# Depthwise convolution of a hybrid trunk step: three channel tiles on VectorE and five on TensorE, with shifted copies of the rows

## What is computed

```python
z = h @ p["w_pw1"] + p["b_pw1"]
a, g = jnp.split(z, 2, axis=-1)
u = a * jax.nn.sigmoid(g)
u = conv_depthwise(u, p["w_dw"], taps=31, padding=15) + p["b_dw"]
u = jax.nn.silu(_layernorm(u, p["ln_g"], p["ln_b"]))
return u @ p["w_pw2"] + p["b_pw2"]
```

## Time and profile before

| | |
|---|---|
| device time, median of 3 runs | 1497.93 us (1497.63 to 1500.12) |
| profiled execution, first to last instruction | 1495.2 us |
| own time of the profiled execution | not given apart; the median is 2.7 us above its span |
| PE busy | 1460.0 us (98%) |
| DVE busy | 1166.2 us (78%) |
| ACT busy | 969.1 us (65%) |
| POOL busy | 39.1 us (3%) |
| DMA, mean over the span | 318 GB/s |

### The profile page before, as it was taken

The page is one execution under the profiler, slowest core; times in us unless marked ns, Lnnn a source line. Parts: engine busy times, 40 slices in busy tenths (PEclk is TensorE's granted clock), DMA queues, the critical chain, the costliest instruction groups (busy, mean ns, idle before and its releaser), DMA issues.

```text
span 1495.2 us, 20201 instructions
## 1 busy us (share of the span) xinstructions
PE 1460.0 (98%) x8274; PEld 1232.3 (82%) x8274; DVE 1166.2 (78%) x1137; ACT 969.1 (65%) x979; POOL 39.1 (3%) x41
## 2 busy tenths in 40 slices
PE   6999999999999999999999999999999999999997
PEld 5778899998977888888888888888888888888885
DVE  3565744455897789889979889878888887988997
ACT  2554633433368487777777778787777777777773
POOL 0210000000000100000000000000000000000010
PEclk9999999999999999999999999999999999999999
DMA  9767766756743579999989999989999998999993
GB/s 375 295 231 281 271 220 231 232 175 226 271 156 109 198 271 375 372 389 377 373 348 378 373 372 392 376 334 389 375 377 385 376 375 347 377 372 389 395 403 140
DMA packets 102530, 474.86 MB, mean 318 GB/s; under 512 B 8316, under 2 KB 39180, under 8 KB 53280
## 3 DMA queue, kind: packets, MB, share of 16 engines
q1 hardware_dynamic: 99696, 465.86, 82.4%
q0 software_dynamic: 2160, 6.92, 1.2%
q10 hardware_dynamic: 576, 0.72, 0.2%
HBM read 468.65 MB, written 4.81 MB: 317 GB/s over the span
## 4 chain that ended last, share of the span: by engine, by line
PE 89%; DVE 5%; DMA 3%; ACT 2%; issue 1%; POOL 0%; ACTq 0%; SPq 0%; DVEq 0%; POOLq 0%
PE bank L1686 20%; PE bank L1684 20%; PE bank L1685 20%; PE bank L1690 6%; PE bank L1692 5%; PE bank L1691 5%; PE bank L2229 2%; PE bank L1727 2%; PE bank L2068 2%; DMA raw<-w_in 1%; PE bank L2022 1%; PE bank L2023 1%; PE bank L2024 1%; DVE hid L1378 1%; PE bank L1744 1%; PE bank L2194 1%
## 5 line engine op out<-in xcount | busy, mean ns | idle before, releaser
L1549 DVE TENSOR_TENSOR low<-raw,high 128x2048 fp32r<-128x2048 f32 x333 | 748.8, 2287 | 106.9 <-ACT high L848 104.9
L848 ACT ACTIVATE high<-raw 128x2048 fp32r<-128x2048 f32 x333 | 632.0, 1921 | 101.5 <-DMA raw<-moe 100.4
L1684 PE MATMUL bank<-high,hidH 128*128 128x512 f32 x896 | 349.5, 390 | 0.0
L1686 PE MATMUL bank<-high,hidL 128*128 128x512 f32 x896 | 349.1, 390 | 0.0
L1685 PE MATMUL bank<-low,hidH 128*128 128x512 f32 x896 | 348.6, 389 | 0.0
L1690 PE MATMUL bank<-hidH,high 128*128 128x256 f32 x736 | 211.5, 287 | 3.4 <-DVE hidL L1013 1.3
L1691 PE MATMUL bank<-hidL,high 128*128 128x256 f32 x736 | 208.1, 283 | 0.0
L1692 PE MATMUL bank<-hidH,low 128*128 128x256 f32 x736 | 208.1, 283 | 0.0
L1686 PEld LDWEIGHTS bank<-high,hidL 128*128 128x128 f32 x896 | 168.2, 188 | 35.0
L1684 PEld LDWEIGHTS bank<-high,hidH 128*128 128x128 f32 x896 | 168.2, 188 | 34.7
L1685 PEld LDWEIGHTS bank<-low,hidH 128*128 128x128 f32 x896 | 168.2, 188 | 34.6
(11 more groups left out here) (244 smaller groups left out, 1292.0 us busy)
## 6 DMA issues: line engine op xcount, KB each, us to landing
raw<-moe SPq DMA_DIRECT2D x336, 1024.0 KB, 5.2
raw<-ada_w SPq DMA_DIRECT2D x40, 1024.0 KB, 5.6
raw<-ffn_gu SPq DMA_DIRECT2D x44, 512.0 KB, 5.0
raw<-ffn_down SPq DMA_DIRECT2D x11, 1024.0 KB, 5.0
raw<-ada_first SPq DMA_DIRECT2D x8, 1024.0 KB, 15.0
raw<-w_in SPq DMA_DIRECT2D x8, 1024.0 KB, 8.7
raw<-conv_pw SPq DMA_DIRECT2D x16, 512.0 KB, 5.1
raw<-w_o SPq DMA_DIRECT2D x4, 1024.0 KB, 6.8
```

The costliest lines, as they stand in the source:

```text
L848: a.activation(high[:, m % SPLITS, :], raw[:, n % RAWS, :], ACT.Copy).then_inc(S("high_ready"), 1)
L1549: v.tensor_tensor(low[:, n % RAWS, :], raw[:, n % RAWS, :], high[:, m % SPLITS, :].bitcast(F32), ALU.subtract).then_inc(S("low_ready"), 1)
L1684: pe.matmul(out, xh, wh, start=start, stop=False)
L1686: return pe.matmul(out, xl, wh, start=False, stop=stop)
```

## The change

- DVE convolves three tiles (DVE_TILES = 3), tiles 0 to 2, and PE five, tiles 3 to 7.
- PE's 128 rows hold four taps of 32 channels. For each tile there are GROUPS = 4 groups of 32 channels and ROUNDS = 8 rounds of four taps. One matmul takes 32 columns of weights and writes the 32 partitions of its group; the four groups of a round write the four quarters of one bank, and the eight rounds sum up. That is 32 matmuls a tile in place of 31, with 32 columns of weights each in place of 128.
- The rows for it lie in `shifted`: for shift a and group g, 32 partitions of `uT` are copied by a DMA to partitions 32a to 32a + 31, moved by a tokens. For each pair of tiles (u = 1, 2, 3; u = 1 has one tile) there are 16 such DMAs, shifts 0 and 1 from ACT's queue and shifts 2 and 3 from POOL's.
- The weights of a tile, 128 x 32 x 32, are made by POOL, one instruction a tile, by multiplying the taps into a 32-column identity (five instructions). They stand in POOL's queue ahead of the four small loads (L478). ACT makes no more diagonal matrices.
- On DVE the taps of two tiles alternate: tiles 0 and 1, then 0 and 2, then 1 and 2. After `glu(2)` there are 14 taps in place of 20.
- `sg` moves into tiles 6 and 7 of `hid`, `uT` to the start of the phase's space with rows of 160, and the ring of diagonal matrices goes.

```diff
-DIAGS = 6
+SHIFTS, GROUPS = 4, 4
+CG = P // GROUPS
+ROUNDS = 8
+UROW = P + 32
...
+DVE_TILES = 3
+PE_TILES = KT - DVE_TILES
...
+        tapU = sb("tapU", [P, 2, GROUPS * ROUNDS, CG], where=ph)
...
+        uT = sb("uT", [P, KT, TILES, UROW], where=ph)
+        shifted = sb("shifted", [P, PE_TILES * GROUPS, TILES, UROW], where=ph)
+        tapD = sb("tapD", [P, 3, GROUPS * ROUNDS, CG], where=ph)
...
+        sg = hid[:, KT - UC:KT, :].rearrange("p c (t n) -> p c t n", t=TILES)
...
+        def conv_tiles(u):
+            return max(UC * u, DVE_TILES) - DVE_TILES, UC * (u + 1) - DVE_TILES
+
+        def shift_rows(eng, u, shifts, arrived):
+            i0, i1 = conv_tiles(u)
+            n = (TILES - 1) * UROW + P + SHIFTS * (ROUNDS - 1)
+            for a in shifts:
+                for g in range(GROUPS):
+                    eng.dma_start(
+                        shifted[CG * a:CG * (a + 1), GROUPS * i0 + g:GROUPS * i1:GROUPS].rearrange(
+                            "c q t n -> c q (t n)")[:, :, 0:n],
+                        uT[CG * g:CG * (g + 1), DVE_TILES + i0:DVE_TILES + i1].rearrange(
+                            "c k t n -> c k (t n)")[:, :, a:a + n]
+                    ).then_inc(S(f"{arrived}{u}"), 16)
...
+            pool.wait_ge(S("state_out"), 32)
+            ident32 = const[:, C_ID32:C_ID32 + CG].unsqueeze(1).to_broadcast([P, GROUPS * ROUNDS, CG])
+            for i in range(PE_TILES):
+                c0 = COLS["tap_groups"][0] + i * GROUPS * ROUNDS
+                w = par[:, c0:c0 + GROUPS * ROUNDS].unsqueeze(2).to_broadcast([P, GROUPS * ROUNDS, CG])
+                st.mark(pool.tensor_tensor(tap_weights(i), w, ident32, ALU.mult), "taps_spread")
             for half, p0 in enumerate((64, 96)):
...
+            for u in range(1, 4):
+                pool.wait_ge(S("glu_ready"), UC * (u + 1))
+                shift_rows(pool, u, (2, 3), "late_shifts")
...
+            def shift_ready(u):
+                a.wait_ge(S("glu_ready"), UC * (u + 1))
+                shift_rows(a, u, (0, 1), "early_shifts")
...
             def conv_out(k):
-                a.wait_ge(S("tap_used"), (k - DVE_TILES + 1) * TAPS)
+                a.wait_ge(S("conv_done"), k - DVE_TILES + 1)
...
+                if u >= 2:
+                    shift_ready(u - 1)
                 glu_gate(u)
-
-            for k in range(DVE_TILES, KT):
-                for j in range(TAPS):
-                    i = (k - DVE_TILES) * TAPS + j
-                    if i >= DIAGS:
-                        a.wait_ge(S("tap_used"), i - DIAGS + 1)
-                    st.mark(a.activation(diag[:, i % DIAGS, :], ident, ACT.Copy,
-                                         scale=taps[:, j * KT + k:j * KT + k + 1]), "diag_ready")
-                if k > DVE_TILES:
-                    conv_out(k - 1)
-                    named("pw2", 0, k - DVE_TILES - 1)
+            shift_ready(3)
+
+            conv_out(DVE_TILES)
+            conv_out(DVE_TILES + 1)
+            named("pw2", 0, 0)
+            conv_out(DVE_TILES + 2)
+            named("pw2", 0, 1)
+            conv_out(DVE_TILES + 3)
             conv_out(KT - 1)
...
+            def conv_taps(k0, j0, k1, j1, n):
+                for j in range(n):
+                    conv_tap(k0, j0 + j)
+                    conv_tap(k1, j1 + j)
...
             glu(0)
-            conv_taps((0, 1), 0, 8)
+            conv_taps(0, 0, 1, 0, 8)
...
             glu(1)
-            conv_taps((0, 1), 8, 16)
+            conv_taps(0, 8, 1, 8, 8)
...
             glu(2)
-            conv_taps((0, 1), 16, 26)
+            conv_taps(0, 16, 2, 0, 7)
             glu(3)
-            conv_taps((0, 1), 26, TAPS)
-            rest = tuple(range(2, DVE_TILES))
-            conv_taps(rest, 0, 8)
+            conv_taps(0, 23, 2, 7, 4)
             rows_out(4)
-            conv_taps(rest, 8, 11)
+            conv_taps(0, 27, 2, 11, 4)
             mod_out(4)
-            conv_taps(rest, 11, 25)
+            conv_taps(1, 16, 2, 15, 6)
             named("pw2", 0, 0)
-            conv_taps(rest, 25, TAPS)
+            conv_taps(1, 22, 2, 21, 9)
+            conv_tap(2, 30)
             named("pw2", 0, 1)
...
+            def conv_tile(k):
+                i, u = k - DVE_TILES, k // UC
+                pe.wait_ge(S("taps_spread"), i + 1)
+                pe.wait_ge(S(f"early_shifts{u}"), 16 * 2 * GROUPS)
+                pe.wait_ge(S(f"late_shifts{u}"), 16 * 2 * GROUPS)
+                if i >= 2:
+                    pe.wait_ge(S("conv_pe_ready"), i - 1)
+                for r in range(ROUNDS):
+                    for g in range(GROUPS):
+                        last = pe.matmul(
+                            bank[CG * g:CG * (g + 1), 4 + k % 2, 0:TOK].rearrange("p (t n) -> p t n", t=TILES),
+                            tap_weights(i)[:, g * ROUNDS + r, :],
+                            shifted[:, GROUPS * i + g, :, SHIFTS * r:SHIFTS * r + P],
+                            start=r == 0, stop=r == ROUNDS - 1)
+                st.mark(last, "conv_done")
...
-            cuts = [(k, j) for k in range(DVE_TILES, KT) for j in range(0, TAPS, 6)]
-            for i, (k, j) in enumerate(cuts):
-                conv_taps(k, j, min(j + 6, TAPS))
-                if i == 5:
-                    ada_sum(4)
-                if i >= 6 and i < 9:
-                    ada_piece(5, i - 6)
+            conv_tile(3)
+            conv_tile(4)
+            ada_sum(4)
+            conv_tile(5)
+            ada_piece(5, 0)
+            ada_piece(5, 1)
+            conv_tile(6)
+            conv_tile(7)
+            ada_piece(5, 2)
             pe.wait_ge(S("conv_part"), DVE_TILES * TAPS)
```

More of the change, by code:

```diff
@@ L54 @@
 C_PAIR = C_SEL + 2 * GC
-C_END = C_PAIR + TILES
+C_ID32 = C_PAIR + TILES
+C_END = C_ID32 + CG
+DVE_TILES = 3
+PE_TILES = KT - DVE_TILES
 COLS = {}
@@ L61 @@
                   ("ln_b", KT), ("w_sc", 3 * SCC), ("q_a", 2), ("kv_a", 1), ("head_gain", 4), ("rope_gain", 4 * ROPE),
-                  ("taps", TAPS * KT), ("router", KT * EXPERTS)):
+                  ("taps", TAPS * DVE_TILES), ("tap_groups", PE_TILES * GROUPS * ROUNDS), ("router", KT * EXPERTS)):
     COLS[_name] = (_c, _c + _n)
@@ L65 @@
 NPAR = _c
-DVE_TILES = 5
 PHASE = 12480
@@ L180, in build @@
         ph.close()
+        ph = ExitStack()
+        tapU = sb("tapU", [P, 2, GROUPS * ROUNDS, CG], where=ph)
+        ph.close()
         sb("up_space", [P, 4 * UC * TOK])
@@ L216, in build @@
         ph = ExitStack()
+        uT = sb("uT", [P, KT, TILES, UROW], where=ph)
+        shifted = sb("shifted", [P, PE_TILES * GROUPS, TILES, UROW], where=ph)
+        tapD = sb("tapD", [P, 3, GROUPS * ROUNDS, CG], where=ph)
+        ph.close()
+        ph = ExitStack()
         sb("row_space", [P, 2 * TILES * D], where=ph)
-        uT = sb("uT", [P, KT, TILES, P + 2 * PAD], where=ph)
-        sg = sb("sg", [P, UC, TILES, P], where=ph)
         sq = sb("sq", [P, KT, TOK], where=ph)
-        diag = sb("diag", [P, DIAGS, P], where=ph)
         ph.close()
@@ L327, in pw2_bank, with tap_weights @@
             return m // 2, (m % 2) * TOK
+        def tap_weights(i):
+            return tapU[:, i] if i < 2 else tapD[:, i - 2]
+        def conv_tiles(u):
[11 more added lines that the diff above has]
+                    ).then_inc(S(f"{arrived}{u}"), 16)
         def kept_rows(e):
@@ L1350, in _ @@
             st.do(v.memset(uT[:, :, :, 0:PAD], 0.0), "pads")
-            st.do(v.memset(uT[:, :, :, PAD + P:], 0.0), "pads")
+            st.do(v.memset(uT[:, :, :, PAD + P:UROW], 0.0), "pads")
             def glu(u):
@@ L1364, in glu, with conv_tap @@
                 v.wait_ge(S("glu_ready"), UC * (u + 1))
[L1366 to L1378, removed]
+            summed = {}
+            def conv_tap(k, j):
+                dst = hid4[:, k, :, :]
+                src = uT[:, k, :, j:j + P]
+                w = taps[:, j * DVE_TILES + k:j * DVE_TILES + k + 1]
+                if j == 0:
+                    b = COLS["dw_b"][0] + k
+                    summed[k] = st.mark(v.tensor_scalar(dst, src, w, par[:, b:b + 1], ALU.mult, ALU.add), "conv_part")
+                else:
+                    v.wait_ge(S("conv_part"), summed[k])
+                    summed[k] = st.mark(v.scalar_tensor_tensor(dst, src, w, dst, ALU.mult, ALU.add), "conv_part")
+            def conv_taps(k0, j0, k1, j1, n):
+                for j in range(n):
+                    conv_tap(k0, j0 + j)
+                    conv_tap(k1, j1 + j)
             named("pw1", "a", 1)
@@ L2332, in constants @@
             c[32 * g + tt, C_PAIR + tt] = 1.0
+        c[32 * g:32 * g + 32, C_ID32:C_ID32 + CG] = np.eye(CG)
     return c
@@ L2373, in parameters @@
     put("rope_gain", np.broadcast_to(np.concatenate(rope)[None, :], (P, 4 * ROPE)))
-    put("taps", columns(inp["conv_dw"][0]))
+    dw = np.asarray(inp["conv_dw"][0], dtype=np.float32)
+    put("taps", columns(dw[:, 0:DVE_TILES * P]))
+    grouped = np.zeros((SHIFTS * ROUNDS, PE_TILES * P), np.float32)
```

(3 more changed lines are left out.)

## The result

| | before | after |
|---|---|---|
| device time, median | 1497.93 us (1496.81 to 1500.12, 5 runs) | 1486.36 us (1483.21 to 1493.24, 5 runs) |
| profiled execution, first to last instruction | 1495.2 us | 1481.4 us |
| start of `ln_sums` | 466.31 us | 451.17 us |
| start of DVE's centring, which waits for it | 469.96 us | 454.93 us |

The ratio is 0.9933, 95% interval 0.9908 to 0.9958. The medians differ by 11.6 us (10.0 by the ratio), where 21.3 were forecast. The sign and the range held, the size did not. In the profiled runs `ln_sums` moved by 15.1 us and the span by 13.8.

What follows compares the result with a forecast made beforehand. All three engines work on the convolution, PE and DVE nearly balanced, memory not the bound. `ln_sums` moves by -23.8 us, POOL's clash adds 2.5, so -21.3: 1497.9 us becomes 1476.6, range 1473 to 1488.

Steps and rivals of the forecast that it cites:

- The sign and the range: Whole kernel: faster by more than 3 us with chance 0.91; range 1473 to 1488 us, about 80%.
- PE's pace: PE's convolution: four column groups run side by side, 0.054 us a record, 17.1 us for 320 records, PE done at 441.1.
- The rivals of 0.068 and 0.11 us: PE's convolution records pack less closely: 0.068 us each gives 1480 us (12%); 0.11 us each gives 1493 us (6%).
- the one on the slower side: PE's column groups don't run side by side: 0.215 us a record, 29 us later, 1527 us; 5%.
- its 1477.9 us: Total if PE's 320 convolution records each took the skill's floor of about 62 ns, 19.8 us together.
- DVE's work: DVE from `glu(3)` done at 419.95 us: 47 taps (18.8 us) and smaller parts, 0.5 us wait included, ending at 442.5.
- The clash with POOL: POOL's five tap-weight instructions (9.0 us) hold up DVE's row work for `pw1`: 2.5 us lost, bounds 0 and 9.0.
- The slack that grows from pair to pair: At the `hidL` pairs for `pw1`: PE's first has no slack, later ones gain 1.2 us a pair.
- 1479.2 us in all: Total in place of 1476.6 if POOL and DVE strictly take turns, the third `hidL` pair some 5.1 us late.
- The copies: 48 added DMAs: u = 3 lands by 429 to 433 us, PE asks at 433.0, so DVE still sets the end.
- The 13% rival: Copies land late (4.2 us) or POOL holds DVE for most of its 9 us (6.5 more): 1481 to 1487 us; 13%.
- -23.8: Forecast move of `ln_sums`, from 466.3 to 442.5 us, before the clash with POOL is added.

Runs made afterwards that it cites:

- the best run with all copies: Changed kernel with tap weights spread later, `ada_sum(4)` ahead of `conv_tile(4)` and the `pw2` 0 0 load behind `ada` 5 3: median 1479.63 us, its profiled run 1474.03.
- its cause put back alone: Kernel with `ada_sum(4)` ahead of `conv_tile(4)` and `pw2` 0 0 behind `ada` 5 3, POOL's tap weights back in the norm instead of later: 1481.86 us.
- One repeated run: The changed kernel measured again unaltered, as control: 1486.95 us (1484.34 to 1491.31), its profiled run 1484.9 us.
- 4.9 and 3.8 us alone, 5.5 together: Against the changed kernel's repeat (1486.95 us): tap weights spread after the norm 1482.02; `ada_sum(4)` ahead of PE's second tile 1483.17; both 1481.49 us.

## Why the prediction was right and wrong

- **PE's pace: right.** 0.055 us a record where 0.054 was forecast. The rivals of 0.068 and 0.11 us, and the one on the slower side, are out. The Trainium skill's floor of 62 ns a matmul (TensorE: Matmul & The Clock Gate, section Wait — 56ns, not 53.3ns?), which it gives for decoding in software, doesn't hold when applied to each record, as the prediction did for its 1477.9 us; whether it would hold for a matmul of two records, here 0.11 us, no run shows.
- **DVE's work: right.** 22.3 us against 22.0 without the wait. From the first step of the norm `ln_sums` comes after 76.6 us without copies and clash, where the forecast makes 76.7, and after 77.3 in the best run with all copies.
- **The clash with POOL: right in mechanism, too small in size.** The step was "I take 2.5 us, nearer to the lower end, for that slack". It measured 4.9 us at `glu(3)`, and 4.9 or 2.2 (centring) and 2.2 (medians) with its cause put back alone. The slack that grows from pair to pair is no help, since the first pair itself came 4.0 us late (ended 368.87 + 3.61 against 367.74 + 0.76), or 4.5 from the first step of the norm. DVE stood for the rest of three POOL instructions and not of one: once in the L1052 pair ahead (1.7 us), and once in each half of the `hidL` pair (2.85 us together). The rule of the Trainium skill (SBUF — State Buffer, section Who interferes with whom), with POOL and DVE taking turns, had given 5.1 us and 1479.2 us in all: the trace agrees with its clash. The prediction counted the `hidL` pairs alone; the L1052 pairs, with one large SBUF input and none in PSUM, stood as well, 1.6 to 1.7 us longer a pair.
- **The copies: this step failed.** "The first two sets are issued while `pw1` still runs and ACT is nearly idle", and after that only the last set was timed. Issued isn't landed. The prediction timed u = 3 at 429 to 433 (it was 439.4, 4.4 us of it from the later `glu(3)`) and left u = 2 out. That set landed by 429.2, up to 10.4 us after the issue, where 5 to 6.6 had been taken for the last one. The price was 4.4 us from `glu(3)` to `ln_sums`. In the profile it stands as 2.3 us of wait and 1.7 of PE at the 1.2 GHz level, which DVE met at `mod_out`; the prediction had looked for such a wait only in front of tile 6. "The idle DMA engines" stood as evidence against lateness, but they were read as a mean over a stretch that starts behind the place. The 13% rival named both costs, 4.2 us for the copies and up to 6.5 more for POOL, and its 1481 to 1487 us is where the median came.
- **The other loads: missed.** `pw2` 0 1 was followed, `pw2` 0 0 was not. ACT had it at 439.23 only, 15.6 us after its issue, and DVE asks for it at 431.6 to 433.7 in the six profiles with neither the clash nor a wait at `mod_out`.
- **The sum.** -23.8, plus 4.9 for the clash, 3.9 for the longer wait at `mod_out` and 0.3 for DVE's work, is -14.7 us, which is the move of `ln_sums` from the first step of the norm (100.5 to 85.8). The profiled run came to that step 0.47 us earlier, which makes the 15.1. Of the centring's 15.0 the span kept 13.8; the last 1.2 us go in the experts' part, between 655 us and the end, and their cause stays open. The median lies 5.0 us above the profiled span and not 2.7: the profiled run was the fastest of five. The other four had spans of 1482.4 to 1491.5 us. One repeated run shows a clock at 1.2 GHz in `ln_sums` and a later `glu(3)`, 2.9 us together at the centring; the cause of the rest of the spread stays open.

## What to carry to other kernels

Read the DMA share where a new transfer is issued and until it is wanted, not as a mean over the stage, and look at what the load queue has sent ahead: small copies that somebody waits for stand behind loads that nobody needs for 20 us. When several waits have one cause, taking them out one at a time gives less than their sum (medians 4.9 and 3.8 us alone, 5.5 together, of 8 to 9 expected); a sign of it is a stall that changes its place. Where profiled runs differ in their start, take times from a step that they share. A load moved forward in a ring takes a slot for longer, so look at who comes seven places behind it.

## What wasn't expected of the hardware

- Copies of 79 KB between partitions took 2.8 (POOL) and 3.1 us (ACT) to land, in the median of the third pair, on a clear queue, and 6.4 and 8.7 behind weight loads, and 8 issues on ACT took 7.06 us (0.6 to 1.67 us each) against 4.35 on POOL.
- In all eight profiles with POOL's work in the norm the granted clock fell to the 1.2 GHz level for 3.4 to 6.8 us near 370 us, behind PE's wait for `hidL`; in none of the seven that moved it away. The clash is paid on PE too: from the first step of the norm to `glu(3)` it is 53.3 to 53.4 us without the clash, 58.1 to 58.2 with it and a dip of 3.4 us, and 58.6 to 58.8 with a dip of 6.8.
- The slowdown goes both ways: POOL's five instructions took 9.8 us beside the norm and 15.7 us where they met DVE's residual parts.
